# Sixteen starting places, changing from chunk to chunk, for the split weights of a transformer kernel

## The reference

```python
# first block
h = rmsnorm(x, g[0]);  proj = h @ w_in            # 2048 x 6736
up = einsum('bsnc,ncd->bsnd', branches, w_branch)  # 3 x (1024 x 2048)
gates = sigmoid(h @ w_gate + b_gate)               # 2048 x 6144
x = x + rmsnorm(sum(gates * up) @ w_out, g[1])
m = square(relu(rmsnorm(x, g[2]) @ w_up)) @ w_down # 2048 x 8192, 8192 x 2048
x = x + rmsnorm(m, g[3])
# second block
p = modulate(rmsnorm(x), silu(c) @ w_ada) @ w_in_2
y = (ga * (attn * silu(z_a)) @ w_pa + gb * (fourier(u_b) * silu(z_b)) @ w_pb) @ w_o
out = rmsnorm(x + gate * y, final_g)
```

## Time and profile before

| what | value |
|---|---|
| median of the 2 runs | 2303.47 us (2302.29 to 2304.64) |
| profiled execution's own time | 2306.96 us |
| its span in the trace | 2305.1 us |
| TensorE matmuls (PE) busy | 2274.0 us, 99% of the span |
| VectorE busy | 1468.4 us, 64% |
| ScalarE busy | 1070.8 us, 46% |
| DMA, mean | 206 GB/s |

### The profile page before, as it was taken

How to read it: one execution, slowest core, us unless ns; L and a number is a source line. 1 busy time by engine, 2 the same in 40 slices (tenths; PEclk the granted TensorE clock), 3 DMA queues, 4 the chain that set the end, 5 groups by cost and what they waited for, 6 DMA issues and landing times.

```text
span 2305.1 us, 37604 instructions
## 1 busy us (share of the span) xinstructions
PE 2274.0 (99%) x15980; PEld 2116.1 (92%) x15980; DVE 1468.4 (64%) x1844; ACT 1070.8 (46%) x1422; POOL 40.4 (2%) x61
## 2 busy tenths in 40 slices
PE   7999999999999999999999999999999999999998
PEld 7889999999999988988988988998889979999987
DVE  6757578787887667544555555555756545577665
ACT  5444435444344456544443443444656545434443
POOL 1000000000000001000000000000100000000000
PEclk9999999999999999999999999999999999999999
DMA  8855676677777765666656656656664444778763
GB/s 273 253 158 163 192 218 222 219 229 240 247 230 251 250 226 176 186 202 192 186 192 192 186 189 197 195 181 209 230 203 132 145 118 139 248 273 274 252 214 138
DMA packets 246368, 473.73 MB, mean 206 GB/s; under 512 B 21166, under 2 KB 25624, under 8 KB 244536
## 3 DMA queue, kind: packets, MB, share of 16 engines
q1 hardware_dynamic: 242888, 454.40, 61.8%
q0 software_dynamic: 3312, 16.92, 2.2%
HBM read 467.05 MB, written 4.21 MB: 204 GB/s over the span
## 4 chain that ended last, share of the span: by engine, by line
PE 95%; DVE 2%; DMA 1%; ACT 1%; issue 1%; POOL 0%; SPq 0%; POOLq 0%; ACTq 0%; DVEq 0%
PE ps L874 19%; PE ps L876 19%; PE ps L875 19%; PE ps L867 10%; PE ps L868 10%; PE ps L869 10%; PE ps L802 1%; PE ps L741 1%; PE ps L663 1%; DMA raw<-in_w_out 1%; PE ps L781 0%; PE ps L791 0%; PE ps L782 0%; DVE tmp L1260 0%; PE ps L637 0%
## 5 line engine op out<-in xcount | busy, mean ns | idle before, releaser
L874 PE MATMUL ps<-op0h,whiW 128*128 128x256 f32 x3248 | 918.5, 283 | 1.1 <-DVE wloW L1234 1.1
L875 PE MATMUL ps<-op0l,whiW 128*128 128x256 f32 x3248 | 910.4, 280 | 0.0
L876 PE MATMUL ps<-op0h,wloW 128*128 128x256 f32 x3248 | 910.3, 280 | 0.0
L1234 DVE TENSOR_TENSOR wloW<-raw,whiW 128x1024 fp32r<-128x1024 f32 (+1 forms) x488 | 591.3, 1219 | 415.5 <-ACT whiW L906 414.0
L906 ACT ACTIVATE whiW<-raw 128x1024 fp32r<-128x1024 f32 (+1 forms) x488 | 512.1, 1056 | 607.5 <-PE ps L876 533.5
L875 PEld LDWEIGHTS ps<-op0l,whiW 128*128 128x128 f32 x3248 | 616.9, 190 | 2.0 <-issue 1.4
L874 PEld LDWEIGHTS ps<-op0h,whiW 128*128 128x128 f32 x3248 | 612.6, 189 | 6.4 <-issue 5.8
L876 PEld LDWEIGHTS ps<-op0h,wloW 128*128 128x128 f32 x3248 | 615.1, 189 | 0.0
L1234 DVE TENSOR_TENSOR wloT<-raw,whiT 128x1024 fp32r<-128x1024 f32 (+1 forms) x280 | 336.2, 1210 | 288.8 <-ACT whiT L906 288.3
L906 ACT ACTIVATE whiT<-raw 128x1024 fp32r<-128x1024 f32 (+1 forms) x280 | 290.8, 1047 | 322.9 <-PE ps L869 269.2
L867 PE MATMUL ps<-whiT,op1h 128*128 128x512 f32 x640 | 249.6, 390 | 0.1
(11 more groups left out here) (264 smaller groups left out, 2114.5 us busy)
## 6 DMA issues: line engine op xcount, KB each, us to landing
raw<-in_w_in SPq DMA_DIRECT2D x256, 512.0 KB, 4.3
raw<-in_w_up SPq DMA_DIRECT2D x128, 512.0 KB, 3.7
raw<-in_w_down SPq DMA_DIRECT2D x128, 512.0 KB, 3.8
raw<-in_w_ada SPq DMA_DIRECT2D x96, 512.0 KB, 4.6
raw<-in_w_gate SPq DMA_DIRECT2D x96, 512.0 KB, 4.6
raw<-in_w_out SPq DMA_DIRECT2D x64, 512.0 KB, 4.4
raw<-in_w_branch SPq DMA_DIRECT2D x48, 512.0 KB, 5.3
raw<-in_w_proj_a SPq DMA_DIRECT2D x24, 512.0 KB, 4.6
```

The lines of the kernel that those rows point to most:

```text
L874: pe.matmul(o, wh, xh[:, ka, :], start=first and m % 2 == 0, stop=False, skip_group_check=True)
L875: pe.matmul(o, wh, xl[:, ka, :], start=False, stop=False, skip_group_check=True)
L876: mm = pe.matmul(o, wl, xh[:, ka, :], start=False, stop=last, skip_group_check=True)
L1234: v.tensor_tensor(wlo[job.mode][q % NSPL][:, :, 0:job.n], x, h.bitcast(F32), ALU.subtract).then_inc(s_lo, 1)
```

## The change

The two views of each buffer, one for each mode, become sixteen views that both modes use. The buffer now begins at a multiple of 256, and the views begin at 0, 16, 32, ... 240 bytes past it. Chunk q uses view number 7q mod 16, so that its start is 112 bytes past that of chunk q - 1, modulo 256. The sixteen starts come round every 16 chunks, in the order 0, 112, 224, 80, 192, 48, 160, 16, 128, 240, 96, 208, 64, 176, 32, 144. Activations, `raw` buffers and everything else stay at the remainders they had. No instruction is added, removed or moved on any engine's queue, and each has the same shape.

```diff
         def split_buffers(name):
-            w = {"T": [], "W": []}
+            w = []
             for i in range(NSPL):
-                o = line(64)
-                for mode, shift in (("T", 0), ("W", 64)):
-                    w[mode].append(at(f"{name}{mode}{i}", [128, KC, 512], o + shift, F32R))
-                top[0] = o + 64 + 4 * KC * 512
+                o = line(0)
+                flat = at(f"{name}{i}", [128, 60 + KC * 512], o, F32R)
+                w.append([flat[:, s:s + KC * 512].rearrange("p (k n) -> p k n", k=KC) for s in range(0, 64, 4)])
+                top[0] = o + 240 + 4 * KC * 512
             return w
...
-                h, l = whi[job.mode][q % NSPL], wlo[job.mode][q % NSPL]
+                h, l = whi[q % NSPL][7 * q % 16], wlo[q % NSPL][7 * q % 16]
...
-                act.activation(whi[job.mode][q % NSPL][:, :, 0:job.n], raw[i][:, :, 0:job.n], ACT.Copy).then_inc(s_hi, 1)
+                act.activation(whi[q % NSPL][7 * q % 16][:, :, 0:job.n], raw[i][:, :, 0:job.n], ACT.Copy).then_inc(s_hi, 1)
...
-                x, h = raw[landed["w", q][0]][:, :, 0:job.n], whi[job.mode][q % NSPL][:, :, 0:job.n]
+                x, h = raw[landed["w", q][0]][:, :, 0:job.n], whi[q % NSPL][7 * q % 16][:, :, 0:job.n]
                 v.wait_ge(s_hi, q + 1)
-                v.tensor_tensor(wlo[job.mode][q % NSPL][:, :, 0:job.n], x, h.bitcast(F32), ALU.subtract).then_inc(s_lo, 1)
+                v.tensor_tensor(wlo[q % NSPL][7 * q % 16][:, :, 0:job.n], x, h.bitcast(F32), ALU.subtract).then_inc(s_lo, 1)
```

## The result

The changed kernel takes 2341.85 us (2341.55 to 2342.15, 2 runs) against 2303.47 us. The ratio is 1.0166, with a 95% interval of 1.0141 to 1.0190: slower by 38 us. The forecast was 2320 us. The time lies within the range of 2272 to 2370 us and on the side that was forecast, but the loss is more than twice the forecast one of 16 us.

A forecast was written before the change was run, and what follows sets the result against it. TensorE's step from one matmul to the next was taken to bound the kernel. Terms 0 + 9.9 + 6.4 = +16.3 us gave 2323.3 us profiled, 2320 us on the median (+0.7%, chance 0.45), range 2272 to 2370 us.

The forecast's parts named there:

- What bounds the kernel: TensorE, busy 99%: only its step between matmuls can move the time; the engines writing split weights wait for it.
- the place does nothing: Rival, chance 0.15: the two speeds come from something other than start places; 2303 us, range 2300 to 2308.
- The first term: ScalarE and VectorE accessing split weights at 16-byte remainders: taken as zero, and hidden by waits for TensorE.
- The second term: Share of chunks unsettled on TensorE: 69% in both modes, so W changes by 0 and T by +9.9 us.
- This case's own range: Forecast's span from half the chunks unsettled (2311 us) to all of them (2334 us).
- none settles: Bound with every TensorE chunk at the slow step: W +16.1 us, T +14.4 us, in sum +30.5 us.
- The third term: TensorE settling anew at each moved start: 27 ns for each of 238 settling chunks, +6.4 us.
- unfavourable distances: Rival, chance 0.22: at some distances TensorE's worst steps last, 9.4 ns a step; 2363 us, range 2330 to 2408.
- most distances settle: Rival, chance 0.13: 64 bytes is the odd distance, any shift frees W's slow stretches; 2280 us, range 2265 to 2295.
- The loss of the settled level: Rival, chance 0.05: even settled TensorE steps' excess over 106.7 and 213.3 ns comes from place and goes; 2251 us or lower.
- the signs that I had named: Profile after: W windows mixed at 115.5 to 118 ns, T near 230 ns, step following q modulo 16, writers' durations unchanged.

The follow-up runs named there:

- run 5: Changed kernel's buffers with fixed starts, activations and weights all 32 bytes further on than in the kernel before, so distances stay: 2303.05 us, ratio 0.9998.
- run 6: Changed kernel's buffers with weights fixed at the old 64 (T) and 128 (W), only the activations' parts moved from 64 to 96: 2344.06 us, ratio 1.0177.
- run 4: Changed kernel with one start kept per mode instead of sixteen, every T chunk at 48 and every W chunk at 176: 2372.47 us, ratio 1.0301.
- run 7: Changed kernel with the same sixteen starts, but each kept for eight chunks: 2339.73 us, ratio 1.0158.
- run 9: Changed kernel's buffers with old fixed starts (T 64, W 128), but the first chunk of each W job begins at 16: 2283.19 us, ratio 0.9912.
- run 10: Changed kernel's buffers with T at 64, W at 128, but W chunks right after a T chunk or side work begin at 16: 2280.30 us, ratio 0.9897.
- run 11: Against run 10, the second W chunk after a sum of 16 small matmuls also begins at 16: 2277.30 us, ratio 0.9883.
- run 8: Changed kernel's buffers, T fixed at 48, W at 128; two of three T products load 64 of 128 weight columns and write 64 rows: 2290.54 us, ratio 0.9943.

## Why the prediction was right or wrong

*What bounds the kernel* held. The writers of the split weights kept their durations (1215 and 1053 ns a piece), and all of the loss lies in TensorE's steps. So did the reading that the two streams' distance sets the step, and that the place has an effect at all. Runs 5 and 6 show both, and the rival "the place does nothing" is out. The Trainium skill's page "TensorE: Matmul & The Clock Gate", part 2, says that loading the next weights takes no SBUF read bandwidth from the running matmul. Read as "so no place costs anything", it disagrees with runs 5 and 6 (2303 and 2344 us, with only the distance of the two operands between them), and the measurement decides. Whether it is read bandwidth that is lost, no run shows.

*The first term*, the writes at 16-byte remainders, was zero, as taken.

*The second term*, the share of unsettled chunks, is the step that failed. I took each distance to be of one of two kinds, settled or 4.5 ns slower, and gave the fourteen unknown ones W's share of before, 69% slow. The runs show no such share. In mode W one place in sixteen settles (128), and the others have cycles of their own with surpluses of 3.4 to 6.6 ns over 113.3. In mode T only 64 reaches the settled step, in the last matmuls of its chunk of 12, and the mean surpluses by place are 2.5 to 8.5 ns over 226.7, 9.7 ns in run 4. So W cost 22 us where I had 0, and T 18 us where I had 9.9. Nor is the surplus the same in both modes, as I had read from 4.5 and 4.4 ns: with both starts fixed it is 6.7 ns in W at 176 and 9.7 in T at 48. I had the bound "none settles" at +30.5 us, and even it was too low, because I had taken the mean of the slow level seen before as the level of all slow distances. This case's own range ended at 2334 us for that reason, and the measured 2342 lies in the stated range only because the price of a rival had widened it.

*The third term*, the price of settling anew at each chunk (6.4 us), was too high: run 7 takes away seven eighths of the changes and gains 2 us. There was little to pay, since there is hardly anything to settle to. The whole surplus over the settled step is 758 x 1.2 ns = 0.9 us at 128 in mode W and 177 x 3.9 ns = 0.7 us at 64 in mode T (steps of those places in the changed kernel, and their means in the table). At 64 in mode T a chunk reaches the settled step only at its end, which costs 12 x 3.9 = 47 ns a chunk, more than the 27 ns that I had taken.

*The rival "unfavourable distances"* was right in its mechanism and too high in its size for the change: a third level that lasts does exist, at the 236 ns that I had read off the settling rows (run 4: 236.4 ns over the program). But I had it as all or half of the chunks; over sixteen places the mean is 232.6 ns. In mode W no place came near the 122.7 ns of this rival; the worst has 120.0. Its point of decision, 2%, was not reached with sixteen starts, and it was with one bad pair of starts, 2372 us.

*The rival "most distances settle"* had one thing right for the wrong reason: to move the start does free W from its slow stretches, if the start comes back to 128 afterwards and stays there (runs 9 to 11). *The loss of the settled level*, 1 in 16, did not go at any place: no place has a mean under 113.3 or 226.7 ns.

As to the signs that I had named: the W windows have a mixture, with 118.3 ns just above the upper edge of 115.5 to 118; T is at 232.8, not near 230; and the step follows q modulo 16.

What stays open: why the two streams meet in such a way, and why a start after the sums or after another T chunk leads to one or the other lasting cycle at 128. The runs show that the distance counts (runs 5 and 6) and so both operands with it, and that a smaller load and result let the surplus go (run 8), but not in what part of the chip the two meet.

## What to carry to other kernels

Where matmuls stand end to end, look at the distance of their starts and not at busy time: here 99% busy hid two speeds 4% apart and a loss of 38 us. This is one kernel with two shapes of matmul, so take it as a thing to measure. With float32r operands that are loaded and streamed at the same time, fix the distance of the two operands' starts modulo 256 for each mode, try the sixteen, and keep it; to spread the starts gives the mean of all, which is worse than a good one. If a good distance has two lasting speeds, see how its stretches are entered: a single chunk at another start was worth 1%.

## What the runs showed of the hardware that was not expected

The steps of TensorE are so regular that one distance gives the same sequence within a nanosecond in most of its chunks. Settled steps are 113.33 and 226.67 ns, which at the granted 2.4 GHz are 272 and 544 cycles for 256 and 512 columns, 17 for each 16. One distance (64 bytes, mode W) has two lasting cycles, 113.3 and 117.8 ns, and each can hold for over 700 matmuls. And half the width of the weight load and of the result, in two of three products, changed a T step of 237.1 to 227.0 ns, 10 ns of a matmul whose own stream was untouched.
